# Six projections of a transformer block by halves with seven products instead of eight, with the sums of the weights on GpSimd

## The reference

```python
h = _rmsnorm(x, g_mix)                         # [256, 1024]
proj = h @ w_in                                # w_in [1024, 7244]
(qa, ka, va, qb, kb, vb, fl, qc, kc, vc, qi, ki, wi, gl) = jnp.split(proj, COL_SPLITS, axis=-1)
br_a = _stick_breaking_attention(heads(qa), heads(ka), heads(va))        # 8 heads of 64 channels
log_f = jax.nn.log_sigmoid(fl + b_forget)
br_b = _forgetting_attention(heads(qb), heads(kb), heads(vb), log_f)     # 8 heads of 64 channels
# qc, kc, qi, ki are rotated by position; each token takes the 64 keys with the highest score of (qi, ki, wi)
br_c = _indexed_sparse_attention(qc, kc, vc, qi, ki, wi, top_k)
gates = jax.nn.sigmoid(gl.reshape(b, s, 3, 1024))
y = gates[0] * (br_a @ w_branch[0]) + gates[1] * (br_b @ w_branch[1]) + gates[2] * (br_c @ w_branch[2])
x = x + y @ w_out
x = x + jnp.square(jax.nn.relu(_rmsnorm(x, g_mlp) @ w_up)) @ w_down
```

## Time and profile before

| | us |
|---|---|
| three runs | 1633.76, 1642.99, 1645.26 |
| their median | 1642.99 |
| the profiled execution, its own time | 1639.52 |
| its span, first to last instruction | 1637.7 |

### The profile page before, as it was taken

The page is one execution under the profiler, slowest core; times in us unless marked ns, Lnnn a source line. Parts: engine busy times, 40 slices in busy tenths (PEclk is TensorE's granted clock), DMA queues, the critical chain, the costliest instruction groups (busy, mean ns, idle before and its releaser), DMA issues.

```text
span 1637.7 us, 29142 instructions
## 1 busy us (share of the span) xinstructions
PE 1573.9 (96%) x12883; PEld 1287.3 (79%) x12883; DVE 655.5 (40%) x1292; ACT 347.1 (21%) x731; POOL 19.3 (1%) x33
## 2 busy tenths in 40 slices
PE   7999999799799899999999999999999999999998
PEld 2544458688688687778788999998777778899998
DVE  2431034555652414223421766521413343176643
ACT  1201132533432302033400121001103340012100
POOL 3000001000000000000000000000000000000000
PEclk9999999899899899999999999999999999999999
DMA  9222240000011524422244444463442224444451
GB/s 350 101 67 87 77 155 3 3 2 18 2 41 67 131 103 154 154 103 103 103 154 154 141 169 155 170 166 112 146 154 104 103 108 149 154 155 155 162 189 49
DMA packets 110894, 191.49 MB, mean 117 GB/s; under 512 B 20889, under 2 KB 27297, under 8 KB 110641
## 3 DMA queue, kind: packets, MB, share of 16 engines
q1 hardware_dynamic: 109776, 188.29, 33.2%
q0 software_dynamic: 960, 1.33, 0.2%
q10 hardware_dynamic: 32, 0.01, 0.0%
HBM read 188.57 MB, written 1.05 MB: 116 GB/s over the span
## 4 chain that ended last, share of the span: by engine, by line
PE 88%; issue 3%; DVE 2%; ACT 2%; PEld 1%; DMA 1%; DVEq 1%; PEldq 1%; ACTq 1%; SPq 0%
PE psum L1255 21%; PE psum L1109 19%; PE psum L1194 10%; PE psum L831 6%; PE psum L1365 5%; PE psum L1117 4%; PE psum L756 4%; PE psum L1300 2%; PE psum L992 2%; PEld psum L1365 1%; PE psum L1380 1%; PE psum L1180 1%; PE psum L1223 1%; DMA arena<-in_x 1%; PE psum L1334 1%
## 5 line engine op out<-in xcount | busy, mean ns | idle before, releaser
L1255 PEld LDWEIGHTS psum<-arena 128*128 128x128 f32 x3136 | 350.5, 192 | 0.1
L1255 PE MATMUL psum<-arena 128*128 128x128 f32 x3136 | 350.5, 275 | 0.0
L1109 PE MATMUL psum<-arena 128*128 128x256 f32 x1440 | 314.2, 379 | 0.0
L1109 PEld LDWEIGHTS psum<-arena 128*128 128x128 f32 x1440 | 272.4, 189 | 40.3 <-issue 1.3
L1784 ACT ACTIVATE arena<-psum 128x512 f32<-128x512 f32 (+6 forms) x246 | 125.8, 517 | 709.2 <-PE psum L1255 176.7
L1194 PE MATMUL psum<-arena 128*128 128x256 f32 x768 | 176.5, 382 | 0.0
L1194 PEld LDWEIGHTS psum<-arena 128*128 128x128 f32 x768 | 141.9, 190 | 26.4 <-issue 5.3
L1365 PE MATMUL psum<-arena 128*128 128x512 f32 (+1 forms) x368 | 139.6, 538 | 1.1 <-issue 1.0
L1365 PEld LDWEIGHTS psum<-arena 128*128 128x128 f32 x368 | 69.3, 190 | 71.5 <-issue 69.0
L831 PE MATMUL psum<-arena 64*64 64x64 f32 x3072 | 96.6, 219 | 2.1 <-issue 2.0
L831 PEld LDWEIGHTS psum<-arena 64*64 64x64 f32 x3072 | 92.6, 134 | 7.5 <-issue 5.3
(11 more groups left out here) (342 smaller groups left out, 1468.2 us busy)
## 6 DMA issues: line engine op xcount, KB each, us to landing
arena<-in_w_in SPq DMA_DIRECT2D x33, 2048.0 KB, 7.8
arena<-in_w_up SPq DMA_DIRECT2D x16, 2048.0 KB, 8.0
arena<-in_w_down SPq DMA_DIRECT2D x16, 2048.0 KB, 7.9
arena<-in_w_out SPq DMA_DIRECT2D x6, 2048.0 KB, 8.0
arena<-in_w_branch SPq DMA_DIRECT2D x6, 2048.0 KB, 7.8
arena<-in_mod_w SPq DMA_DIRECT2D x5, 2048.0 KB, 14.0
arena<-in_w_in SPq DMA_DIRECT2D x3, 1024.0 KB, 6.7
arena<-in_w_in SPq DMA_DIRECT2D x12, 256.0 KB, 4.8
```

The source lines that it names most:

```text
L1109: mm = pe.matmul(b[:, i * T:(i + 1) * T], w[:, k, c:c + P], src[:, k, :], start=k == 0, stop=k == ks - 1)
L1255: mm = pe.matmul(b[:, n * P:(n + 1) * P], left[:, k, n * P:(n + 1) * P], right[:, k, :], start=first and n == 0 and k == 0, stop=last and ...
```

## The change

Each of the six projections is cut into halves in all three dimensions: weights into w11, w21, w12, w22 (rows by columns), tokens into x11, x12, x21, x22, and the result into c11, c12, c21, c22. Seven products of sums and differences take the place of eight. A product is a PSUM group of its own, 128x256, `qa_1` to `qa_7`, taken in the order 1, 6, 7, 5, 2, 3, 4. PE has for q and k 56 matmuls with 128 columns moving in a chunk, and for v 28 matmuls with 256 columns moving.

- DVE makes four sums of the tokens (t1 to t4), once a layer, before anything else of its work there.
- GpSimd makes the sums of the weights for each chunk: s1, s2, w11 - w21 (in place) and s4, each 128x1024, in two buffers used in turn. Its sums of chunk i wait for that chunk's weights and for the last product of chunk i - 2. PE waits for the first three sums ahead of product 6, for the fourth ahead of product 3.
- ACT copies product 1 of each part out of PSUM. DVE adds the other six to it in seven instructions (`head_added`).
- DVE's work is put in a new order around these: ropes (all PSUM reads first), qa, forget gates, ka, scores, va, 2 rounds of the search, qb, 3 rounds, kb, 3 rounds and `bias_c`, vb, and then attention as before.
- The factor 0.125 of the B branch moves from ACT's copy of qb to DVE's masked scores; the forget sums are scaled by -8 instead of -1.
- PE waits ahead of z0 for five `heads_added` (before: for ACT's copy of `vb1`), and ahead of o0 for six.

```diff
-    p += [(f"{x}{n}", "A", 1) for x in ("qa", "ka") for n in range(2)] + [(f"dot{n}", "A", 2) for n in range(2)]
-    p += [(f"{x}{n}", "A", 1) for x in ("va", "qb", "kb", "vb") for n in range(2)]
+    for x in HEAD_PARTS:
+        if x == "va":
+            p += [(f"dot{n}", "A", 2) for n in range(2)]
+        p += [(f"{x}_{m}", "A" if m == 1 else "D", 1) for m in HEAD_PRODUCTS]
...
+                for l in range(LAYERS):
+                    if l:
+                        ly.wait_emptied(gp, "br23", l - 1)
+                    for i in range(len(HEAD_PARTS)):
+                        n = len(FIRST) + 3 + i
+                        gp.wait_ge(s_slot[SLOT[n]], l * SLOT_PER_LAYER[SLOT[n]] + landed(n))
+                        if i >= 2:
+                            ly.wait_filled(gp, f"{HEAD_PARTS[i - 2]}_4", l)
+                        s1, s2, s4 = [head_sums[:, i % 2, x] for x in range(3)]
+                        w11, w21, w12, w22 = quarters(ring[:, SLOT[n]])
+                        gp.tensor_tensor(s1, w21, w22, ALU.add)
+                        gp.drain()
+                        gp.tensor_tensor(s2, s1, w11, ALU.subtract)
+                        gp.tensor_tensor(w21, w11, w21, ALU.subtract)
+                        gp.drain().then_inc(sem("head_weights_summed"), 1)
+                        gp.tensor_tensor(s4, w12, s2, ALU.subtract)
+                        gp.drain().then_inc(sem("head_weights_summed"), 1)
...
+            def head_product(b, x, i, w, m):
+
+                s1, s2, s4 = [head_sums[:, i % 2, y] for y in range(3)]
+                w11, w21, w12, w22 = quarters(w)
+                x11, x12, x21, x22 = token_halves(ht)
+                t1, t2, t3, t4 = [tok1[:, y] for y in range(4)]
+                left, right = {1: (w11, x11), 6: (s2, t2), 5: (s1, t1), 7: (w21, t3), 2: (w12, x21), 3: (s4, x22), 4: (w22, t4)}[m]
...
+                if x[0] == "v":
+                    for k in range(half):
+                        mm = pe.matmul(b[:, 0:T], right[:, k, :], left[:, k, :], start=k == 0, stop=k == half - 1)
+                    return mm
+                for n in range(2):
+                    for k in range(half):
+                        mm = pe.matmul(b[:, n * P:(n + 1) * P], left[:, k, n * P:(n + 1) * P], right[:, k, :], start=k == 0, stop=k == half - 1)
+                return mm
...
-                for n in range(2):
-                    if x[0] == "v":
-                        tokens(f"{x}{n}", w, 0, 512, n)
-                    else:
-                        tiles(f"{x}{n}", w, (2 * n * P, (2 * n + 1) * P))
+                for m in HEAD_PRODUCTS:
+                    head_product(take_bank(ly, f"{x}_{m}", l), x, i, w, m).then_inc(ly.filled, 1)
...
+                ly.wait_emptied(dve, f"{x}_1", l)
+                emptied(ly, dve.tensor_tensor(c12, p(6), c11, ALU.add))
+                fence()
+                emptied(ly, dve.tensor_tensor(c21, p(7), c12, ALU.add))
+                fence()
+                p5 = p(5)
+                dve.tensor_tensor(c22, p5, c21, ALU.add)
+                emptied(ly, dve.tensor_tensor(c12, p5, c12, ALU.add))
+                fence()
+                emptied(ly, dve.tensor_tensor(c11, p(2), c11, ALU.add))
+                emptied(ly, dve.tensor_tensor(c12, p(3), c12, ALU.add))
+                emptied(ly, dve.tensor_tensor(c21, c21, p(4), ALU.subtract))
+                done("heads_added")
```

More of the change, by code:

```diff
@@ L368 @@
 PLAN_END = [(f"fin{m}{n}", "D") for m in range(2) for n in range(2)]
[L370 removed]
+CHUNK_ENDS = (["qc1", "qi", "fl"] + [f"{x}_4" for x in HEAD_PARTS] + [f"gl{2 * n + 1}" for n in range(6)]
               + [f"br{b}3" for b in range(3)] + ["out1", "out3"] + [f"up{2 * n + 1}" if n < FIRST_SEVEN else f"up{n}_4" for n in range(8)]
@@ L1214, in layer_tensor @@
                     b = take_bank(ly, f"o{i - 1}", l)
+                    if i == 1:
+                        pe.wait_ge(sem("heads_added"), len(HEAD_PARTS) * (l + 1))
                     ly.wait_emptied(pe, f"wT{i - 1}", l)
@@ L1542, in layer_scalar @@
                     done("dots_ready")
[L1543 to L1548, removed]
+                ly.wait_filled(act, f"{x}_1", l)
+                b = bank(ly, f"{x}_1", l)[:, 0:T]
+                emptied(ly, copy(head_quarters(x, dst)[0], b if x[0] == "v" else blocks_of(b)))
             def weights_out(i):
@@ L2304, in layer_vector, with head_added, p @@
             fence()
+            x11, x12, x21, x22 = token_halves(ht)
+            t1, t2, t3, t4 = [tok1[:, n] for n in range(4)]
+            dve.tensor_tensor(t1, x12, x11, ALU.subtract)
+            fence()
+            dve.tensor_tensor(t2, x22, t1, ALU.subtract)
+            dve.tensor_tensor(t3, x22, x12, ALU.subtract)
+            fence()
+            dve.tensor_tensor(t4, t2, x21, ALU.subtract)
+            done("token_sums1")
+            def head_added(x, dst):
+                c11, c12, c21, c22 = head_quarters(x, dst)
+                def p(m):
+                    ly.wait_filled(dve, f"{x}_{m}", l)
+                    b = bank(ly, f"{x}_{m}", l)[:, 0:T]
+                    return b if x[0] == "v" else blocks_of(b)
+                ly.wait_emptied(dve, f"{x}_1", l)
+                emptied(ly, dve.tensor_tensor(c12, p(6), c11, ALU.add))
+                fence()
+                emptied(ly, dve.tensor_tensor(c21, p(7), c12, ALU.add))
+                fence()
+                p5 = p(5)
+                dve.tensor_tensor(c22, p5, c21, ALU.add)
+                emptied(ly, dve.tensor_tensor(c12, p5, c12, ALU.add))
+                fence()
+                emptied(ly, dve.tensor_tensor(c11, p(2), c11, ALU.add))
+                emptied(ly, dve.tensor_tensor(c12, p(3), c12, ALU.add))
+                emptied(ly, dve.tensor_tensor(c21, c21, p(4), ALU.subtract))
+                done("heads_added")
             ly.wait_filled(dve, "wi", l)
@@ L2340, in layer_vector, with search @@
             dve.tensor_tensor(wk, score, cst("causal"), ALU.add)
-            for _ in range(TOPK // 8):
-                fence()
-                for m, o, w in tiles:
-                    dve.max(top8[:, m, :], wk[:, o:o + w])
-                fence()
-                for m, o, w in tiles:
-                    dve.match_replace(wk[:, o:o + w], top8[:, m, :], wk[:, o:o + w], TAKEN)
+            def search(n):
+                for _ in range(n):
+                    fence()
+                    for m, o, w in tiles:
+                        dve.max(top8[:, m, :], wk[:, o:o + w])
+                    fence()
+                    for m, o, w in tiles:
+                        dve.match_replace(wk[:, o:o + w], top8[:, m, :], wk[:, o:o + w], TAKEN)
+            for x, dst, n in (("va", va, 2), ("qb", qb, 3), ("kb", kb, TOPK // 8 - 5)):
+                head_added(x, dst)
+                search(n)
             fence()
```

42 lines of the change are left out of this document (29 added, 13 removed).

## The result

| | before | changed |
|---|---|---|
| median, us | 1639.59 (4 runs, 1633.76 to 1645.26) | 1619.89 (4 runs, 1616.66 to 1623.69) |
| the profiled execution, us | 1639.52 | 1622.89 |
| its span, us | 1637.7 | 1621.1 |
| six projections to the first z, layer 0 / layer 1, us | 85.49 / 85.49 | 76.04 / 76.04 |

The ratio is 0.9883, with a 95% interval of 0.9854 to 0.9913. A second measurement beside the last experiments gave 0.9897 (0.9883 to 0.9910). One execution of experiment 7 ran at a mean granted clock of 0.841 and took 1839.10 us; that experiment's median counts it, its ratio does not.

What follows compares the result with a forecast made beforehand. PE, busy for 96% of the span, was taken as the bound. Saving 9.6 us a layer, 19.2 for two, gave 1620.3 us, or 1623.8 on the median's terms; the forecast was 1622 us, range 1610 to 1640.

Steps and rivals of the forecast that it cites:

- The sum of the prediction: Whole kernel: 1639.52 us less 19.2 us for two layers gives 1620.3 us on the profiled execution's terms.
- The saving of PE: Six projections: q and k 5.53, v 3.38, wait ahead of z0 0.69; together 9.6 us a layer.
- GpSimd's price: Weight sums on GpSimd: 0.94 to 2.8 us each, 2.8 taken, with no wait for PE.
- The recurrence: GpSimd's sums over six chunks: no PE wait up to 3.3 us each, 8 us a layer at 4.0.
- DVE's time table: DVE's work beside the projections: `bias_c` done at 687.8 us, vb's additions at 694.4, all hidden behind PE.
- The margin at ka_7: PE's product ka_7 needs a PSUM bank that DVE empties; some 9 us to spare.
- The rival of GpSimd and DVE stopping each other: GpSimd's running sums block DVE instructions with two SBUF operands, up to 11.3 us a chunk; strong form 1646 us, chance 0.08.
- the mild form: GpSimd's sums hold up DVE's scores but not its search; qb_7 waits 0.9 us; held likelier than the strong form.
- only the scores are hit: DVE's scores held up by GpSimd: va's additions start at 660.9 us, qb_7, due at 660.4, waits 0.9 us.
- DVE waiting for PE in each `heads_added`: Sign that the forecast is right: DVE's additions of each projection's products wait for PE.
- The rival of GpSimd's pace: PE waits for weight sums at product 6, va to vb; at 5.0 us a sum 1672 us; chance 0.09.
- The other rivals: Semaphores halve the gain, 1629 us, 0.09; attention gives back up to 4 us a layer, 0.05; PE's stream not shorter, 0.02.

Runs made afterwards that it cites:

- experiment 7: Kernel before, with GpSimd also making the weight sums, which nobody reads: 1639.65 us, ratio 1.0004 to the kernel before.
- Experiment 1: Changed kernel with only q and k by halves, va and vb as before: 1629.89 us, ratio 0.9939 to the kernel before.
- experiments 2: Changed kernel with two of GpSimd's four sums made twice, six a chunk: 1624.04 us, ratio 0.9903 to the kernel before.
- experiment 8: Changed kernel with GpSimd's sums doubled to eight a chunk from va on only: 1671.68 us, ratio 1.0203 to the kernel before.
- experiment 9: Changed kernel with GpSimd's sums for ka delayed to run beside DVE's ropes: 1627.41 us, ratio 0.9934 to the kernel before.
- experiment 3: Changed kernel with all four GpSimd sums made twice, eight in every chunk: 1683.45 us, ratio 1.0260 to the kernel before.
- experiment 4: Changed kernel with the whole search and `bias_c` in one piece ahead of va's additions: 1645.12 us, ratio 1.0028 to the kernel before.
- experiment 5: Changed kernel with the whole search and `bias_c` in one piece behind va's additions: 1628.14 us, ratio 0.9921 to the kernel before.
- experiment 6: Changed kernel with DVE making the weight sums too, GpSimd none: 1618.72 us, ratio 0.9872 to the kernel before; repeated, 1620.09 us.

## Why the prediction was right

**The time.** The sum of the prediction was 1620.3 us, and 1622 us was put on record because the profiled execution lay under the median of three runs. With a fourth run that median came down to 1639.59, the profiled execution's own level, and the measured 1619.89 is at the sum. That it agrees to 0.4 us is partly luck: the four executions of the changed kernel lie up to 7 us apart, and the profiled one, 1622.89, has the 2.3 us ahead of qa.

**The saving of PE** was forecast at 9.6 us a layer and measured at 9.45; the stretch at 75.9 us and measured at 76.04. The rate of the products by halves elsewhere in the kernel held for these to 0.1%: the 224 records of qb and kb take 684.13 - 659.12 = 25.01 us, 0.1117 each. (Those of qa and ka, up to the start of the dots, take 25.10, as 27.82 stood beside 27.74 before.) v's records are at 0.218 instead of 0.2173. Experiment 1 shows the two terms apart: q and k 5.4 us (forecast 5.53), v with the wait 4.05 (forecast 4.07).

**GpSimd's price** was bounded between 0.94 and 2.8 us, and I took 2.8; it is 2.0 to 2.4. Taking three passes at the memset's pace was too dear, on the safe side of the decision. The recurrence was tested in experiments 2 and 8: right for GpSimd's part at six instructions (1.5 us against 1.6), a few us too high at eight (14.9 against 19.3).

**DVE's time table** held: the last additions of vb end at 696.9 us in a run that is 2.27 us late as a whole, that is 694.6 against the 694.4 forecast, in spite of 11 us of hold-ups in between that I had left out of the sum. They fell where the margins were; the sum had no term for them, only the rival below, so that part is luck and not foresight. By the end of `bias_c` DVE was 0.4 us later than forecast (690.50 - 2.27 = 688.2 against 687.8). The margin at ka_7, "some 9", is 9.1 by experiment 9.

**The rival of GpSimd and DVE stopping each other** was right as a mechanism. I held the mild form likelier because the search reads one operand, and the search did keep its pace. In the place of "only the scores are hit" the forget gates are hit too. The condition that I gave, two operands from SBUF, was too narrow: the tensor-scalar instructions, which read one tensor, were held up as well. And the scores lost 6.0 us instead of up to 11.3, so va's additions started at 657.70 - 2.27 = 655.4 us instead of 660.9, and qb_7 didn't wait. They then ran through without waiting for PE, so that the sign "DVE waiting for PE in each `heads_added`" failed at va. The Trainium skill, "SBUF — State Buffer", section "SBUF: two separate sides", says that a DVE operation with two SBUF inputs, or in a 2-port mode, and a GpSimd operation that reads SBUF exclude each other for a whole instruction. The trace agrees: 0.42 us became 2.18 for an instruction with two SBUF inputs (L2405), the two tensor-scalar instructions of the scores went from 0.55 us to 4.46 (L2420), and those with one input from PSUM (0.42 us, L2373) and the search's MAX8 and MATCH_REPLACE8 (0.41 us) didn't change. What decides whether it costs anything is where it falls: 11 us in the changed kernel for nothing, 11.5 us on the ropes for 4.1 us in one layer and 2.6 in the other (experiment 9), 20 us on the ropes for some 14 (experiment 3).

**The rival of GpSimd's pace** did not come. At twice the work it did, and the kernel was slower by 2.0 to 2.6%. The price that I had worked out for it, waits alone, was too low: behind the 14.9 us of waits a layer in experiment 8 there were 7.8 us of slower records.

**The other rivals** did not come either. Semaphores of 42 groups at 0.1 us each would have made 4.2 us a layer; the rate above leaves nothing for them. DVE starts the first masked scores 697.96 - 696.33 = 1.63 us after z0, as before (705.14 - 703.51), and from the first z of layer 0 to qa of layer 1 both kernels take 444.06 us (1147.57 - 703.51 and 1140.39 - 696.33), so attention gives nothing back.

**What the prediction didn't ask** is what of DVE's new order matters. With the sums on GpSimd, that the search no longer stands ahead of va's additions is worth 11.5 us a layer (experiment 4), more than the whole gain; that it is split into 2, 3 and 3 rounds 2 us (experiment 5). Both prices include a hold-up by GpSimd; without it they were not measured. That GpSimd makes the sums is worth nothing here (experiment 6): DVE's 76 us have room for all of them.

## What to carry to other kernels

Where one engine is the bound at full share, an algebraic saving on it is worth its own rows' rate times the count, and the work goes into finding, for each PSUM bank and each sum, who must have been there and by when; the margins (9 to 12 us here) are then the real result. An engine at rest is not free to use: ask which instructions of its neighbour run at the same time and what waits behind them. Before giving work to a slower engine, lay it into the gaps of the faster one: here that gave the same time.

## What I had not expected of the hardware

- A wait of PE can cost more than itself, since the records behind it are slower while the granted clock is below 1. Behind waits of 3.6, 4.6, 4.9, 5.2, 6.5, 8.7 and 11.0 us this was 1.9, 2.8, 2.8, 2.2, 3.1, 2.7 and 3.1 us more (experiments 8, 4 and 3). The missing share of the clock accounts for it: (1 - 0.89) x 24.06 = 2.6 us behind 8.7 us, (1 - 0.81) x 15.64 = 3.0 behind 6.5, (1 - 0.86) x 12.42 = 1.7 behind 3.6. Behind 2.4 us it was 1.7 us in one layer (clock 0.86) and 0.3 in the other, behind 1.9 us 0.3, both at a clock of 1.00, so these 0.3 us are not the clock's; behind 1.5 us nothing (48 records of 256 columns in 10.6 us, as in the earlier trace rows). Length alone doesn't order them, and these runs don't tell what else does.
- GpSimd's four sums are alike in size and not in time: s2 = s1 - w11, whose first operand is contiguous, takes 2.00 us, the other three, whose first operand is a half of the ring's rows, 2.35 us. No run tells the operand apart from the rest.
- GpSimd is held up as well, but less: w11 - w21 of va, across DVE's forget gates, took 2.74 us instead of 2.35.
